# A pair's value row is added one pair later on VectorE, behind the dots of the next pair

## Chip, cores and metric

One core of one Trainium2 chip. The metric is the device time of one execution in microseconds (us); a kernel's time is the median of its runs.

## The reference

One layer over 512 latent tokens of width 1024 (and 256 context tokens): a token mixer, then an expert mixer (PEER). All in float32. The change lies in the expert mixer, whose core is, for each block of 128 tokens `xb`:

```python
q = (xb @ w_q).reshape(T, 8, 2, 128)
s = jnp.einsum('thpd,hpnd->thpn', q, keys)      # scores against 2 x 128 keys for each of 8 heads
sv, si = lax.top_k(s, 16)
cand = sv[:, :, 0, :, None] + sv[:, :, 1, None, :]
cv, ci = lax.top_k(cand.reshape(T, 8, 256), 16)
eid = i1 * 128 + i2                             # i1, i2: taken from si by ci // 16 and ci % 16
g = jax.nn.softmax(cv, axis=-1)
u = jnp.take(u_tab, eid, axis=0)
act = jax.nn.gelu(jnp.einsum('thkd,td->thk', u, xb))
out = jnp.einsum('thk,thkd->td', g * act, jnp.take(v_tab, eid, axis=0))
```

So each token picks 8 x 16 = 128 experts. Of each it needs a row `u` (1024 numbers), dotted with the token, and a row `v`, added to the output with the weight gate x gelu(dot). The block is followed by a norm, a scaling and the residual.

## The kernel before

**Tiling.** The 512 tokens are four blocks t of 128, one token on each of the 128 partitions. A step n from 0 to 511 is one expert of each token of a block (128 steps in a block). A pair j = 0 to 255 is the steps 2j (even) and 2j + 1 (odd). `BT` = 64 pairs make a block, `BP` = 16 pairs make a group of two heads.

**Gathers.** The tables u and v lie side by side in memory, so that GpSimd's one indirect DMA for a step (L613) fetches row u and row v of each of the 128 tokens: 8 KB on each partition, 1.049 MB in all. They go into a ring of six slots (`NGS`, `gslot`), step n into slot n % 6; the ring holds three pairs. GpSimd issues the steps in order. Before step n it waits until the row of step n - 6 in its slot is used up: for an even step on `s_vadd` (VectorE has added that row, L612), for an odd one on `s_peused` (TensorE has multiplied it).

**One pair, engine by engine.** VectorE (`pick(j)`) waits for the landing of each row (`landed`) and takes its dot with the token (L1642), one instruction for a row. ScalarE (its own `pick(j)`) waits for both dots, takes gelu (L1128), multiplies by the gate into `wexp` (L1133, two instructions), and builds a diagonal matrix from the odd step's weight (L1138). TensorE (`add_row`, L917) multiplies the odd row v by that matrix in four column pieces and sums over the block in two banks. VectorE waits for the even step's weight (`s_wexp`) and adds the even row v times the weight to `vacc` (L1657; L1654 for the first of a block). The even values are thus summed by VectorE, the odd ones by TensorE. At the end of a block `products(t)` adds the two sums: ScalarE copies TensorE's sums to `vbuf` (L1145), VectorE adds `vacc` (L1668).

**Ranking.** The next groups' experts are picked by VectorE in small steps. `rank(g)` is a generator; `pick(j)` takes four of its steps in each of the first 12 pairs of a group of 16, between the dots and the add, for the group two further on. No group is left to be ranked from pair 240 on.

**Order.** A list `BSEQ` is written out ahead, and each engine runs its own part of each entry in that order: ("pk", j) is a pair, and behind it, for j below 112, stand side steps: the query projections of the expert mixer (L887, with ScalarE's copies L1101 and others) and the late half of the token mixer (L671, L707, L856), whose weights SyncE loads through a ring of four buffers. ScalarE and TensorE too take all of this in order, so that a pair can stand behind a side step. From pair 112 on there are only pairs, ranking and the ends of blocks.

Of the kernel before, what the change touches and what calls it, by code (L numbers as in the profile page):

```python
# [28 lines left out]
def build(nc, x, ctx_in, rows_a, rows_b, w_ada, w_in, w_dt, conv_w, dt_bias, a_log, d_skip, w_out, w_q, keys,  # L29
# [110 lines left out]
    BT = NE // 2  # L140
# [105 lines left out]
    with ExitStack() as stack:  # L246
# [180 lines left out]
        def landed(eng, n):  # L427
            eng.wait_ge(s_gsl[n % NGS], 16 * (n // NGS + 1))

        def row_u(n):  # L430
            return gslot[n % NGS][:, 0:D]

        def row_v(n):
            return gslot[n % NGS][:, D:2 * D]
# [765 lines left out]
        def _(dve):  # L1200
# [12 lines left out]
            def link(ins):  # L1213

                post(ins)
                settle()
# [418 lines left out]
            def pick(j):  # L1635

                nonlocal ranking
                t = j // BT
                for n in (2 * j, 2 * j + 1):
                    landed(dve, n)  # L1640
                    k = n % NE
                    V.tensor_tensor_reduce(row_u(n), row_u(n), h2[t], 1.0, 0.0, ALU.mult, ALU.add,  # L1642
                                           dots[:, k:k + 1]).then_inc(s_dot, 1)
                g = j // BP + 2
                if j % BP < 12 and g < len(groups):
                    if j % BP == 0:
                        ranking = rank(g)
                    for _ in range(4):
                        next(ranking, None)
                n = 2 * j  # L1650
                w = wexp[:, n % NE:n % NE + 1]
                dve.wait_ge(s_wexp, n + 1)
                if j % BT == 0:
                    V.tensor_scalar(vacc, row_v(n), w, None, ALU.mult).then_inc(s_vadd, 1)  # L1654
                else:
                    dve.wait_ge(s_vadd, j)
                    V.scalar_tensor_tensor(out=vacc, in0=row_v(n), scalar=w, in1=vacc,  # L1657
                                           op0=ALU.mult, op1=ALU.add).then_inc(s_vadd, 1)
# [4 lines left out]

            def products(t):

                dve.wait_ge(s_vcp, t + 1)
                dve.wait_ge(s_vadd, (t + 1) * BT)
                link(V.tensor_tensor(vbuf, vbuf, vacc, ALU.add))  # L1668
# [20 lines left out]
            def late_squares(ct):  # L1689
# [3 lines left out]
                else:  # L1693
                    dve.wait_ge(s_sqaB, ct)
                    V.tensor_tensor(sqacc[1], sqacc[1], sq[1], ALU.add).then_inc(s_sqaB, 1)

            parts = {"rank": rank_end, "norm": gate_norm, "pk": pick, "vs": products, "fin": finish,
                     "zy": late_z, "gn": group_scale, "conv": lambda ct: conv(ct, 1),
                     "gate": lambda ct: gated(ct, 1), "sqa": late_squares, "yT": y_drain, "ss": lambda: sc_sum(1),
# [48 lines left out]
```

## Time and profile before

| | us |
|---|---|
| runs of the kernel | 2097.53, 2096.0, 2109.05 |
| median | 2097.53 |
| profiled execution: first to last instruction (span) | 2089.7 |
| VectorE busy | 1491.0 (71%) |
| TensorE matmul busy | 1518.5 (73%) |
| GpSimd busy | 878.6 (42%) |
| ScalarE busy | 497.1 (24%) |

The profiled execution's own device time is not listed apart from its span; the nearest of the runs, 2096.0, is 6.3 us above that span. The share of busy time is a mean over very different stages: the mixer up to about 583 us, then the expert phase. "Idle before" in a row of the page is the time in which the engine did nothing just ahead of such an instruction, with what ended most of it. Busy time of the DMA engines is a share of all 16.

### The profile page before, as it was taken

What the parts mean: (1) busy time and instruction counts of PE and PEld (TensorE: products, weight loads), DVE (VectorE), ACT (ScalarE), POOL (GpSimd) and SP (SyncE); (2) the same over time, 40 slices, a digit from 0 to 9 for tenths busy, and PEclk for the clock granted to TensorE, in tenths of its full rate; (3) what the DMA queues carried; (4) which work ended last, traced back from release to release, by engine and by line L of the source; (5) the groups of instructions that cost most, each with busy time, mean ns of one, the idle gap of its engine ahead of it and who ended that gap; (6) DMA issues with size and microseconds to landing.
All of it is one profiled execution on the core that took longest, in us unless ns stands there. A gap on an engine that the chain in (4) does not pass through costs nothing.

```text
span 2089.7 us, 15934 instructions
## 1 busy us (share of the span) xinstructions
PE 1518.5 (73%) x4648; PEld 876.7 (42%) x4648; DVE 1491.0 (71%) x2906; ACT 497.1 (24%) x1412; POOL 878.6 (42%) x658
## 2 busy tenths in 40 slices
PE   7899999889667778887865778655555555556564
PEld 3465787668545555564531445311111111111111
DVE  2545368763276667878598856688898898898876
ACT  2201120111222233223233322222222223222222
POOL 2478404220033333343345434345554555455553
PEclk9899899999879899999987899877777767676677
DMA  8233221124278999999999999799999999999997
GB/s 348 101 139 138 89 79 61 62 77 144 81 308 353 362 351 345 410 392 387 421 393 361 386 378 347 282 413 387 413 412 422 403 409 387 409 417 409 406 418 294
DMA packets 90604, 647.28 MB, mean 310 GB/s; under 512 B 10413, under 2 KB 10773, under 8 KB 12565
## 3 DMA queue, kind: packets, MB, share of 16 engines
q0 software_dynamic: 76448, 555.78, 66.7%
q1 hardware_dynamic: 13376, 90.25, 11.2%
q8 instruction: 38, 0.62, 0.1%
q14 instruction: 49, 0.40, 0.1%
q10 hardware_dynamic: 693, 0.23, 0.0%
HBM read 644.12 MB, written 2.10 MB: 309 GB/s over the span
## 4 chain that ended last, share of the span: by engine, by line
PE 42%; DMA 21%; DVE 19%; issue 8%; ACT 7%; POOL 2%; SPq 0%; DVEq 0%; ACTq 0%; POOLq 0%
DMA arena<-in_peer_uv,arena 21%; PE bank L917 13%; PE bank L671 11%; DVE arena L1642 6%; PE bank L887 6%; PE bank L856 4%; DVE arena L1657 3%; PE bank L707 3%; POOL arena L613 2%; ACT smalls L1138 2%; ACT arena L1133 1%; ACT arena L1128 1%; PE bank L906 1%; PE bank L697 1%; PE bank L800 1%
## 5 line engine op out<-in xcount | busy, mean ns | idle before, releaser
L613 POOL DMA_INDIRECT arena<-in_peer_uv,arena x512 | 688.8, 1345 | 901.4 <-DVE arena L1657 571.1
L917 PE MATMUL bank<-arena,smalls 128*128 128x512 f32 x1024 | 700.9, 822 | 477.6 <-ACT smalls L1138 470.7
L1642 DVE CUSTOM_DVE_ANT_0 arena<-arena 128x1024 f32<-128x1024 f32 x512 | 615.1, 1221 | 87.5 <-DMA arena<-in_peer_uv,arena 86.1
L917 PEld LDWEIGHTS bank<-arena,smalls 128*128 128x128 f32 x1024 | 225.7, 241 | 887.8 <-ACT smalls L1138 675.2
L1657 DVE SCALAR_TENSOR_TENSOR arena<-arena 128x1024 f32<-128x1024 f32 x252 | 322.0, 1278 | 204.8 <-ACT arena L1133 204.8
L671 PE MATMUL bank<-arena 128*128 128x256 f32 (+1 forms) x1216 | 336.1, 433 | 3.6 <-ACT arena L962 3.4
L671 PEld LDWEIGHTS bank<-arena 128*128 128x128 f32 x1216 | 235.9, 195 | 104.6 <-issue 76.0
L1128 ACT ACTIVATE arena<-arena 128x2 f32<-128x2 f32 x256 | 51.9, 203 | 778.0 <-DVE arena L1642 776.3
L887 PE MATMUL bank<-arena 128*128 128x256 f32 x512 | 125.4, 402 | 0.7 <-issue 0.7
L1133 ACT ACTIVATE arena<-arena 128x1 f32<-128x1 f32 x512 | 122.9, 287 | 8.5
L887 PEld LDWEIGHTS bank<-arena 128*128 128x128 f32 x512 | 106.2, 208 | 35.9 <-issue 21.5
L856 PE MATMUL bank<-arena 128*128 128x256 f32 x512 | 114.5, 382 | 1.9 <-DVE arena L1493 1.6
L856 PEld LDWEIGHTS bank<-arena 128*128 128x128 f32 x512 | 98.1, 192 | 23.3 <-issue 10.7
L1138 ACT ACTIVATE smalls<-ident,arena 128x128 f32<-128x128 f32 x256 | 102.8, 401 | 8.4
L533 POOL TENSOR_TENSOR arena<-arena,cs 128x2048 f32<-128x2048 f32 x16 | 58.3, 3641 | 52.0 <-PE bank L679 43.2
L1280 DVE TENSOR_SCALAR arena<-bank,early 128x512 f32<-128x512 f32 (+1 forms) x28 | 18.4, 693 | 82.3 <-PE bank L671 82.3
L1262 DVE SCALAR_TENSOR_TENSOR arena<-bank,early,arena 128x496 f32<-128x496 f32 (+1 forms) x112 | 62.6, 622 | 0.6
L707 PE MATMUL bank<-arena 128*128 128x256 f32 x256 | 60.9, 398 | 0.0
L707 PEld LDWEIGHTS bank<-arena 128*128 128x128 f32 x256 | 52.1, 204 | 12.3 <-issue 5.0
L556 POOL TENSOR_TENSOR arena<-arena 128x256 f32<-128x256 f32 x7 | 5.4, 776 | 95.2 <-DVE arena L1394 95.2
L968 ACT ACTIVATE arena<-arena 128x512 f32<-128x512 f32 x16 | 10.1, 630 | 148.1 <-DVE arena L1262 148.1
L1500 DVE TENSOR_TENSOR arena<-bank,arena 128x512 f32<-128x512 f32 x8 | 5.5, 688 | 54.6 <-ACT arena L1058 54.6
(241 smaller groups left out, 1311.5 us busy)
## 6 DMA issues: line engine op xcount, KB each, us to landing
arena<-in_w_in SPq DMA_DIRECT2D x40, 1024.0 KB, 6.2
arena<-in_w_ada POOLq DMA_DIRECT2D x16, 1024.0 KB, 5.1
arena<-in_w_out SPq DMA_DIRECT2D x16, 1024.0 KB, 6.8
arena<-in_peer_w_q SPq DMA_DIRECT2D x16, 1024.0 KB, 9.9
arena<-in_w_ada SPq DMA_DIRECT2D x8, 1024.0 KB, 9.2
arena<-in_peer_uv,arena POOLq DMA_INDIRECT x512
arena<-in_x SPq DMA_DIRECT2D x4, 512.0 KB, 11.3
out<-arena SPq DMA_DIRECT2D x4, 512.0 KB
```

The costliest lines, as they stand in the source:

```text
L613: nc.gpsimd.indirect_dma_start(gslot[n % NGS], None, uv_tab[0], bass.IndirectOffsetOnAxis(eid[t % 2][:, k:k + 1], 0)).then_inc(s_gsl[n % N ...
L671: last = mm(dst, w[:, k, j * P:(j + 1) * P], hT(k), start=(k == 0), stop=(k == KD - 1))
L707: last = mm(ps[:, i * WCOL:(i + 1) * WCOL], hT_tile(halves[half][i], k), w[:, k, :], start=(k == 0), stop=(k == KD - 1))
L856: last = mm(ps[:, i * WCOL:(i + 1) * WCOL], src[:, k, i * P:(i + 1) * P], w[:, k, :], start=(k == 0), stop=(k == KD - 1))
L887: last = mm(ps[:, i * WCOL:(i + 1) * WCOL], h2T[:, m % NA, k, :], w[:, k, :], start=(k == 0), stop=(k == KD - 1))
L917: last = mm(acc[h][:, :], diag[:, j % NDG], row_v(n)[:, h * 512:(h + 1) * 512], start=(i == 0), stop=(i == BT - 1))
L1128: A(gelu[:, k:k + 2], dots[:, k:k + 2], ACT.Gelu_apprx_tanh).then_inc(s_gelu, 1)
L1133: A(wexp[:, k + i:k + i + 1], gate[t % 2][:, k + i:k + i + 1], ACT.Copy, scale=gelu[:, k + i:k + i + 1]).then_inc(s_wexp, 1)
L1138: A(diag[:, j % NDG], ident[:], ACT.Copy, scale=wexp[:, k + 1:k + 2]).then_inc(s_diag, 1)
L1262: return V.scalar_tensor_tensor(out=d, in0=s, scalar=w, in1=d, op0=ALU.mult, op1=ALU.add)
L1642: V.tensor_tensor_reduce(row_u(n), row_u(n), h2[t], 1.0, 0.0, ALU.mult, ALU.add, dots[:, k:k + 1]).then_inc(s_dot, 1)
L1657: V.scalar_tensor_tensor(out=vacc, in0=row_v(n), scalar=w, in1=vacc, op0=ALU.mult, op1=ALU.add).then_inc(s_vadd, 1)
```

## The change

In `pick(j)` of VectorE the last part, the wait for the weight and the add of the even value row, becomes a function of its own, `add_value(j)`. `pick(j)` calls it for the pair before, j - 1, behind its own dots and ranking steps; the first pair of a block calls nothing. The last pair of a block is added at the start of `products(t)`. The arithmetic and the other engines' programs stay as they are.

```diff
                         ranking = rank(g)
                     for _ in range(4):
                         next(ranking, None)
+                if j % BT:
+                    add_value(j - 1)
+
+            def add_value(j):
+
                 n = 2 * j
                 w = wexp[:, n % NE:n % NE + 1]
                 dve.wait_ge(s_wexp, n + 1)
...
             def products(t):
 
+                add_value((t + 1) * BT - 1)
                 dve.wait_ge(s_vcp, t + 1)
                 dve.wait_ge(s_vadd, (t + 1) * BT)
                 link(V.tensor_tensor(vbuf, vbuf, vacc, ALU.add))
```

## Rows read from the trace of the kernel before

**Rows 1.** The page: the DMA share in 40 slices (tenths), and two costly groups.
```profile
DMA  8233221124278999999999999799999999999997
L613 POOL DMA_INDIRECT arena<-in_peer_uv,arena x512 | 688.8, 1345 | 901.4 <-DVE arena L1657 571.1
L1657 DVE SCALAR_TENSOR_TENSOR arena<-arena 128x1024 f32<-128x1024 f32 x252 | 322.0, 1278 | 204.8 <-ACT arena L1133 204.8
```

**Rows 2.** Stage windows: start:end, length, each engine's busy us (instructions), clock, DMA share, GB/s.
```profile
core 0: us, PE busy (x) PEld busy (x) DVE busy (x) ACT busy (x) POOL busy (x), PEclk, DMA share, GB/s
583.00:1348.00 765.00, 574.64 (x1896) 365.17 (x1896) 557.68 (x1130) 220.78 (x622) 305.46 (x233) 0.89 0.94 369
1348.00:2078.00 730.00, 425.42 (x565) 132.90 (x564) 624.49 (x1196) 184.16 (x602) 383.08 (x280) 0.72 0.99 405
900.00:1050.00 150.00, 121.88 (x433) 81.49 (x432) 112.57 (x233) 40.23 (x124) 53.28 (x46) 0.94 0.99 408
```

**Rows 3.** Windows of L1642 alone (two records a dot), then of L1657 alone.
```profile
583.00:1348.00 765.00, 274.26 (x459) 0.89 0.94 369
1348.00:2078.00 730.00, 343.78 (x566) 0.72 0.99 405
1348.00:2078.00 730.00, 177.72 (x140) 0.72 0.99 405
```

**Rows 4.** Waits in 1350 to 2078 us: total us, times, longest.
```profile
POOL arena L613 <- DVE arena L1657: 220.0, 128, 4.9
POOL arena L613 <- PE bank L917: 84.3, 76, 2.2
DVE arena L1642 <- DMA arena<-in_peer_uv,arena: 60.8, 93, 2.2
DVE arena L1657 <- ACT arena L1133: 38.4, 64, 0.7
```

**Rows 5.** Waits in 583 to 1350 us.
```profile
DVE arena L1657 <- ACT arena L1133: 166.4, 67, 9.2
ACT arena L1101 <- PE bank L887: 115.4, 14, 9.5
```

**Rows 6.** Timeline of the last pairs: start, length, instruction, [idle before, releaser].
```profile
2062.79 1.28 DVE L1657 SCALAR_TENSOR_TENSOR arena<-arena 128x1024 f32<-128x1024 f32 x1 [0.60 <-ACT arena L1133]
2064.35 1.68 POOL L613 DMA_INDIRECT arena<-in_peer_uv,arena  x1 [1.34 <-DVE arena L1657]
2065.92 1.23 DVE L1642 CUSTOM_DVE_ANT_0 arena<-arena 128x1024 f32<-128x1024 f32 x1 [0.70 <-DMA arena<-in_peer_uv,arena]
2067.23 0.94 POOL L613 DMA_INDIRECT arena<-in_peer_uv,arena  x1 [1.21 <-PE bank L917]
2075.95 1.22 DVE L1642 CUSTOM_DVE_ANT_0 arena<-arena 128x1024 f32<-128x1024 f32 x1 [0.61 <-DMA arena<-in_peer_uv,arena]
2081.11 1.23 DVE L1668 TENSOR_TENSOR arena<-arena 128x1024 f32<-128x1024 f32 x1 [2.05 <-ACTq L1147]
```

**Rows 7.** The chain of waits, 1500 to 1530 us: start, length, what.
```profile
1505.21 9.45 DMA arena<-in_peer_uv,arena
...
1521.03 8.65 DMA arena<-in_peer_uv,arena
```

**Rows 8.** An issue with idle DMA engines (timeline), and windows behind it (POOL only).
```profile
1336.03 1.68 POOL L613 DMA_INDIRECT arena<-in_peer_uv,arena  x1 [4.88 <-DVE arena L1657]
...
1335.00:1338.00 3.00, 1.68 (x1) 1.00 0.00 0
1338.00:1339.00 1.00, 0.95 (x1) 1.00 0.73 131
1338.00:1344.60 6.60, 2.93 (x3) 1.00 0.84 310
```

**Rows 9.** A quick issue, its first bytes, and the last bytes of all (as rows 8).
```profile
1312.30 0.94 POOL L613 DMA_INDIRECT arena<-in_peer_uv,arena  x1 [6.34 <-DVE arena L1657]
...
1313.00:1314.00 1.00, 0.25 (x1) 0.50 0.24 41
2075.00:2076.00 1.00, 0.00 (x0) 0.50 0.02 8
```

## The prediction

> **What bounds the kernel now.** I read the page first: the busy shares by slice, then the costliest groups [rows 1]. From slice 12 on the DMA engines are at nine or ten tenths, and what they carry is the 512 indirect gathers. The same page says that GpSimd, which issues them, sat idle 901.4 us in front of them and that 571.1 us of this ended with VectorE's value add (L1657). So the add is not just arithmetic: it hands back the slot into which the next gather goes. Then the stage windows [rows 2]. The expert phase has two parts: one in which other projections run beside it (583 to 1348 us) and one of gathers alone (1348 to 2078 us). In the second the DMA share is 0.99 at 405 GB/s; VectorE is busy 624.5 of 730 us, 86%. There are 283 dots in it [rows 3], 141.5 pairs, so a pair takes 730 / 141.5 = 5.16 us; two gathers of 1.049 MB at 405 GB/s take 5.18 us. **The second part runs at the speed of the transfers**, with VectorE close behind. The first part has 229 dots, 114.5 pairs of 6.68 us.
>
> The waits of the second part [rows 4] say what the change can remove: VectorE's add waits 38.4 us for ScalarE's weight, 0.6 us at a time, and this time is idle time of an engine that next waits 60.8 us for a landing. Taking 38 us out of it makes the other wait longer. In the first part the add waits 166.4 us [rows 5].
>
> **How deep the queue is.** The timeline of the last pairs [rows 6] is plain enough to number the gathers backwards from 511. Gather 510 (even, the next to last) is issued at 2064.35, 0.28 us after the end of the add of pair 252 (2062.79 + 1.28), whose even slot it takes. The odd one, 511, is issued at 2067.23 and its dot starts at 2075.95, having waited for it: 8.7 us. The chain of waits shows the same stretch elsewhere, issue to odd dot, at 9.45 and 8.65 us [rows 7]. What would it be with nothing ahead in the queue? At 1336.03 a gather is issued while the engines stand still [rows 8]. They stay at 0.00 until 1338 and are at 0.73 in the next microsecond: about 2.2 us of start-up (I count from 1338.25). A transfer is 2.6 us, and from the last bytes, somewhere in 2075 to 2076 at a share of 0.02 [rows 9], to the dot are some tenths; with the thin tail before them I count 0.7 us. Together 5.5 us. So an odd gather has 8.7 - 5.5 = 3.2 us to spare. Even 510 has landed by 2075.9 less one transfer, 2073.3, which is 9.0 us after its issue and leaves 3.5 us.
>
> **The change, part by part.** No instruction is added or removed: 256 adds stay 256. What moves is the order on VectorE.
> - The add of pair j now stands behind both dots of pair j+1 and the ranking steps put there. Add 252 (2062.79 to 2064.07) would come behind the odd dot of pair 253, which starts at 2065.92 because it waits for a landing: it would end at 2065.92 + 1.23 + 1.28 = 2068.43, **4.36 us later**, more where ranking steps stand between. Spare are 3.2 to 3.5 us. The slot comes back too late, by about 1 us even with no ranking, and the cover that now hides the whole latency of a gather is gone. Of six slots (three pairs) one pair more is held.
> - Queued behind it: the gather of an even row waits for this add on GpSimd's queue, and the odd row's gather stands behind it in that queue. TensorE has released the odd slot long before, which now helps nothing: POOL's 84.3 us behind L917 [rows 4] turn into waits for L1657.
> - VectorE's wait for the weight goes to about nothing, since ScalarE has the next two dots' time for it. Worth 0: late next is the landing.
> - At three block ends and at the very end the last add is done in `products`, behind the one that is late: one add (1.28 us) more there, 4 times 1.28 = 5 us without cover. The cover is ScalarE's copy of TensorE's sums, for which VectorE stood idle 2.05 us before it summed `vbuf` at 2081.11 [rows 6]: 0.
> - ScalarE and TensorE keep their order. The dots come before the add now, so ScalarE gets them 1.9 us sooner where data has already landed; in the second part it has not.
>
> **The sum, second part.** The new loop spans two pairs: landing of the odd row of j+1, its dot, ranking, add j, issue for pair j+3, transfer, landing of j+3. Terms: dot 1.23 [rows 6]; ranking 0.73 (VectorE's busy 624.5 less dots 343.8 less adds 177.7 [rows 2, 3] is 103.0, over 141.5 pairs, block ends counted in); add 1.28; GpSimd's answer 0.28; start-up 2.2; two transfers at 405 GB/s 5.18; notice 0.7. Sum 11.60 us for two pairs, **5.80 us a pair**. Start-up, which the present loop hides, is bounded from both sides. After the quick issue of 1312.30 (0.94 us long) first bytes come at about 1313.76, a share of 0.24 in that microsecond [rows 9]: 1.46 us, and 5.43 us a pair. After the slow issue of 1336.03 (1.68 us) the bytes of both rows are in at 1344.6, 8.6 us, where start-up and two transfers at full rate would be 7.4 [rows 8]: engines that ran dry climb slowly. With that the two pairs take 12.8 us, 6.41 us each. I take 5.85: GpSimd's issue will stand beside VectorE's next dot, as at 1336.03, so the slow start is the nearer row, but at 6.41 us the engines would hardly run dry and there would be little to climb. Cost: (5.85 - 5.16) x 141.5 = **98 us**, ends 38 and 177.
>
> That fixed part has a page too. The Trainium skill, DMA: Bandwidth & Descriptors, section Anatomy of one DMA, fits a DMA issued by GpSimd as 2.0 us plus its bytes at 436 GB/s. An estimate from it is 4.4 us for one gather, against the 5.5 above, and the loop would be about 5.3 us a pair, near rival 1. The rows show more than 2.0 us for start-up alone after a slow issue, so I go by them.
>
> **First part.** Per pair 6.68 us, and weights share the engines. In 900 to 1050 us the share is 0.99 with 46 gathers [rows 2], 23 pairs of 6.5 us; 408 GB/s x 150 us less 48.2 MB of rows leaves 13 MB, 0.54 weight loads a pair. Over two pairs that is 2.8 us of DMA, half of it inside the loop: 11.6 + 1.4 = 13.0, 6.5 us a pair. The loop is as long as the pair already is: uneven pairs lose, the mean hardly. Where TensorE and ScalarE set the pace (the engines stand idle from 1335 to 1338 [rows 8]), gathers land early and a late release costs nothing. I take 0.25 us on 114.5 pairs: **29 us**, ends 0 and 80 (0.7 us, what the second part loses).
>
> Sum: 98 + 29 = 127 us on the profiled span of 2089.7, 2217. The runs lie 6.3 us and more above that span, the median 7.8 above; so 2097.5 + 127 = **2225 us**.
>
> **Rivals.**
> 1. *The fixed part of a gather is smaller (no change).* With start-up at 1.46 and notice at 0.2, the loop is 1.23 + 0.73 + 1.28 + 0.28 + 1.46 + 5.18 + 0.2 = 10.36, 5.18 us a pair: nothing is lost, and the time stays at 2097 to 2100. For: the quick start of rows 9, and the 9.45 us of rows 7, which leave 4.0 to spare. Against: the 8.65 beside it, the slow issue beside a dot, and ranking in 12 of 16 pairs. The Trainium skill's fit, named above, comes within 0.1 us a pair of this.
> 2. *Faster: VectorE's waits were on the path.* In the first part L1657 waits 166.4 us for ScalarE [rows 5], up to 9.2 us. With dots ahead of the add, gelu, diagonal and TensorE's product come sooner. If a quarter of the 166.4 shortens the path and the second part holds, 2097.5 - 42 = 2056. It decides if the loop over two pairs stays under 10.3 us (2 x 5.16). Against: the long waits are ScalarE standing behind TensorE's query halves in its own order (ACT L1101 waits 115.4 us for L887), which dots done sooner don't move.
> 3. *Every pair pays the ramp, the first part too.* 177 + 80 = 257: 2355 us. Against: a loop that long no longer runs dry.
> 4. *The change doesn't do what it says.* Only if the order of the dots and the add came out as before; the add is a call behind the ranking steps, so it does not. No chance of its own.
>
> **How the numbers follow.** Forecast (a loop of 5.4 to 6.4 us a pair in the second part, some loss in the first) 0.80; rival 3 or beyond 0.09; rival 1 0.07; rival 2 0.04. Low: 38 + 0 gives 2135, taken as 2130. High: the second part's upper end and half of the first's, 177 + 40, gives 2315, taken as 2320. One per cent, 21 us, is about what a measurement here can tell from no change. Faster by over 1% 0.04, within 1% 0.07, slower by over 1% 0.89.
>
> **What would show it.** In the second part: a pair every 5.8 us; DMA share near 0.88 instead of 0.99 and GB/s near 360; GpSimd's wait for L1657 up from 220 us toward 350 and its wait for L917 gone; VectorE's wait for the landing (L1642) up from 61 us to some 150, its wait for ScalarE gone; issue to odd dot near 6 us rather than 8.7 to 9.5. In the first part: a span from 765 to about 795 us. The prediction is wrong if the DMA share of the second part stays at 0.99, or if the first part takes most of the loss.

## The result: 2391 us, 14% slower

| kernel | median us | runs | ratio to before (95% interval) |
|---|---|---|---|
| before | 2096.8 | 2092.9 to 2109.05 | |
| with the change | 2391.2 | 2384.6 to 2399.2 | 1.1395 (1.1354 to 1.1437) |

The forecast was 2225 us, the range 2130 to 2320. The sign and the place were right. The size was not: 294 us lost, where 127 were forecast and 223 were the most that the range allowed.

The page of the changed kernel (the group's fields are as in [rows 1]; the add is now L1662):

```profile
DMA  8243212242898988898889888888888888888886
q0 software_dynamic: 76448, 555.78, 62.6%
L613 POOL DMA_INDIRECT arena<-in_peer_uv,arena x512 | 620.0, 1211 | 1267.3 <-DVE arena L1662 1041.0
L1642 DVE CUSTOM_DVE_ANT_0 arena<-arena 128x1024 f32<-128x1024 f32 x512 | 625.1, 1225 | 549.2 <-DMA arena<-in_peer_uv,arena 547.2
L1662 DVE SCALAR_TENSOR_TENSOR arena<-arena 128x1024 f32<-128x1024 f32 x252 | 321.4, 1276 | 6.2 <-ACT arena L1133 5.8
```

Nothing is dearer on VectorE (the add 1276 ns, before 1278). Its wait for ScalarE fell from 204.8 to 5.8 us, and its wait for landings, 60.8 us in the second part before [rows 4], is 547.2 us over the whole kernel. GpSimd waits 1041.0 us for the add instead of 571.1 [rows 1].

By parts, in windows of the same columns as [rows 2]. Pair 112 starts its dots at 1406.5 us here, at 1335.7 us before; the last pair at 2374.8 and 2074.1.

```profile
583.00:1411.00 828.00, 599.70 (x1870) 373.27 (x1869) 558.11 (x1127) 216.47 (x608) 270.08 (x228) 0.84 0.88 335
1411.00:2378.00 967.00, 493.67 (x596) 156.11 (x594) 638.19 (x1211) 188.32 (x613) 349.90 (x285) 0.65 0.85 311
```

The second part's DMA share is 0.85 at 311 GB/s, against 0.99 at 405. TensorE's granted clock fell too, from 0.72 to 0.65, while TensorE was busy for 51% of the second part instead of 58%. With the dots' starts as marks, the time went here:

| | pairs | us a pair before | after | us in all |
|---|---|---|---|---|
| up to the first dot | | | | +4.1 |
| first part | 112 | 6.65 | 7.24 | +66.7 |
| second part | 143 | 5.16 | 6.77 | +229.9 |

Together 300.7 of the 301.4 us between the two spans. The waits of the second part, beside [rows 4]:

```profile
POOL arena L613 <- DVE arena L1662: 547.6, 138, 7.5
DVE arena L1642 <- DMA arena<-in_peer_uv,arena: 315.4, 220, 4.0
POOL arena L613 <- issue: 38.7, 127, 0.3
```

GpSimd's wait for TensorE is gone from the list, as forecast; the odd gather follows the even one at once. So TensorE's lower clock holds up no gather here. The timeline shows the loop over two pairs, at a pair without ranking steps (rows between left out):

```profile
2253.62 1.23 DVE L1642 CUSTOM_DVE_ANT_0 arena<-arena 128x1024 f32<-128x1024 f32 x1 [2.46 <-DMA arena<-in_peer_uv,arena]
...
2254.77 1.28 DVE L1662 SCALAR_TENSOR_TENSOR arena<-arena 128x1024 f32<-128x1024 f32 x1
...
2256.32 0.95 POOL L613 DMA_INDIRECT arena<-in_peer_uv,arena  x1 [4.35 <-DVE arena L1662]
...
2257.57 1.78 POOL L613 DMA_INDIRECT arena<-in_peer_uv,arena  x1 [0.30 <-issue]
...
2259.76 1.23 DVE L1642 CUSTOM_DVE_ANT_0 arena<-arena 128x1024 f32<-128x1024 f32 x1 [1.21 <-DMA arena<-in_peer_uv,arena]
...
2264.75 1.23 DVE L1642 CUSTOM_DVE_ANT_0 arena<-arena 128x1024 f32<-128x1024 f32 x1 [2.57 <-DMA arena<-in_peer_uv,arena]
...
2267.23 1.23 DVE L1642 CUSTOM_DVE_ANT_0 arena<-arena 128x1024 f32<-128x1024 f32 x1 [1.25 <-DMA arena<-in_peer_uv,arena]
```

The odd dot at 2253.62 belongs to some pair j + 1. The add of pair j follows it, the even gather of pair j + 3 goes out at 2256.32, 2.7 us behind the dot's start, and the odd dot of pair j + 3 starts at 2267.23, having waited: 10.9 us behind the issue. Two pairs took 13.6 us. At 2259.76, 3.4 us after that issue, the pair j + 2, issued one turn earlier, has only just come in. Over pairs 112 to 239 (up to 240 a later group is still ranked, in 12 pairs of each 16) the timeline gives, as means, 3.53 us from odd dot to even issue, the release, and 10.07 us from even issue to odd dot, the delivery: 13.6 us, 6.81 us a pair. With six slots in this order the two add up to two pair times by the way they are counted, so the sum is no test; what moves each of them is.

### The profile page after: what moved, and what is told of

Read it like the earlier page. It is cut to its first block, busy times and chain, and to the rows that moved or that the text cites. A ratio compares the mean times of both kernels' runs of the same rounds, so it can differ in the third digit from the quotient of the medians.

```text
span 2391.1 us, 15934 instructions
## 1 busy us (share of the span) xinstructions
PE 1615.3 (68%) x4648; PEld 909.8 (38%) x4648; DVE 1503.3 (63%) x2906; ACT 497.5 (21%) x1412; POOL 809.8 (34%) x658
## 3 DMA queue, kind: packets, MB, share of 16 engines
q0 software_dynamic: 76448, 555.78, 62.6%
## 4 chain that ended last, share of the span: by engine, by line
DMA 40%; PE 24%; DVE 18%; issue 9%; POOL 6%; ACT 3%; POOLq 0%; SPq 0%; DVEq 0%; ACTq 0%
DMA arena<-in_peer_uv,arena 39%; PE bank L671 10%; POOL arena L613 6%; DVE arena L1662 5%; PE bank L917 4%; DVE arena L1642 3%; PE bank L856 2%; PE bank L887 2%; PE bank L707 1%; PE bank L697 1%; DVE arena L1602 1%; PE bank L800 1%; DVE arena L1233 1%; PE bank L786 1%; PE bank L636 1%
## 5 line engine op out<-in xcount | busy, mean ns | idle before, releaser
L917 PE MATMUL bank<-arena,smalls 128*128 128x512 f32 x1024 | 787.2, 912 | 682.0 <-ACT smalls L1138 681.8
L613 POOL DMA_INDIRECT arena<-in_peer_uv,arena x512 | 620.0, 1211 | 1267.3 <-DVE arena L1662 1041.0
L1642 DVE CUSTOM_DVE_ANT_0 arena<-arena 128x1024 f32<-128x1024 f32 x512 | 625.1, 1225 | 549.2 <-DMA arena<-in_peer_uv,arena 547.2
L917 PEld LDWEIGHTS bank<-arena,smalls 128*128 128x128 f32 x1024 | 251.0, 268 | 1146.8 <-ACT smalls L1138 916.4
L1662 DVE SCALAR_TENSOR_TENSOR arena<-arena 128x1024 f32<-128x1024 f32 x252 | 321.4, 1276 | 6.2 <-ACT arena L1133 5.8
L671 PEld LDWEIGHTS bank<-arena 128*128 128x128 f32 x1216 | 238.3, 197 | 107.4 <-issue 77.9
L887 PE MATMUL bank<-arena 128*128 128x256 f32 x512 | 128.6, 409 | 0.7 <-issue 0.7
L887 PEld LDWEIGHTS bank<-arena 128*128 128x128 f32 x512 | 108.4, 212 | 37.1 <-issue 21.7
L856 PE MATMUL bank<-arena 128*128 128x256 f32 x512 | 115.3, 383 | 1.9 <-DVE arena L1493 1.6
L856 PEld LDWEIGHTS bank<-arena 128*128 128x128 f32 x512 | 99.0, 194 | 24.6 <-issue 11.9
L1262 DVE SCALAR_TENSOR_TENSOR arena<-bank,early,arena 128x496 f32<-128x496 f32 (+1 forms) x112 | 62.6, 621 | 0.6
L707 PE MATMUL bank<-arena 128*128 128x256 f32 x256 | 62.6, 406 | 0.0
L707 PEld LDWEIGHTS bank<-arena 128*128 128x128 f32 x256 | 53.3, 208 | 13.3 <-issue 5.5
L1642 DVE DVE_READ_ACCUMULATOR2_ANT arena<- 128x1 f32 x512 | 42.3, 83 | 0.0
L968 ACT ACTIVATE arena<-arena 128x512 f32<-128x512 f32 x16 | 10.1, 631 | 148.2 <-DVE arena L1262 148.2
```

The costliest lines, as they stand in the source:

```text
L613: nc.gpsimd.indirect_dma_start(gslot[n % NGS], None, uv_tab[0], bass.IndirectOffsetOnAxis(eid[t % 2][:, k:k + 1], 0)).then_inc(s_gsl[n % N ...
L671: last = mm(dst, w[:, k, j * P:(j + 1) * P], hT(k), start=(k == 0), stop=(k == KD - 1))
L707: last = mm(ps[:, i * WCOL:(i + 1) * WCOL], hT_tile(halves[half][i], k), w[:, k, :], start=(k == 0), stop=(k == KD - 1))
L856: last = mm(ps[:, i * WCOL:(i + 1) * WCOL], src[:, k, i * P:(i + 1) * P], w[:, k, :], start=(k == 0), stop=(k == KD - 1))
L887: last = mm(ps[:, i * WCOL:(i + 1) * WCOL], h2T[:, m % NA, k, :], w[:, k, :], start=(k == 0), stop=(k == KD - 1))
L917: last = mm(acc[h][:, :], diag[:, j % NDG], row_v(n)[:, h * 512:(h + 1) * 512], start=(i == 0), stop=(i == BT - 1))
```

## The experiments

Theory A is the prediction's: the slot comes back too late, too few gathers are under way, and two pairs take release plus delivery. Rival B: the new order itself costs, through ScalarE, TensorE or slower transfers, however early slots come free. Every kernel's second part is described by two numbers from its timeline, the time of a pair (from the start of pair 112's even dot to the last pair's) and the delivery, the mean time from a pair's even issue to its odd dot over pairs 112 to 239. Where a time of a pair is called one of pairs 112 to 239, it is the mean over the same pairs. Each of these numbers is from one profiled execution.

**1. Ranking behind the add.** In the changed kernel:

```diff
+                if j % BT:
+                    add_value(j - 1)
                 if j % BP < 12 and g < len(groups):
                     ...
                         next(ranking, None)
-                if j % BT:
-                    add_value(j - 1)
```

> The changed order, but the four ranking steps of a pair stand behind the add of the pair before: dots j, add j-1, ranking j. Theory A (the release of the even slot is late, and two pairs take the path from the odd dot to the gather's issue, 3.53 us as measured in the changed kernel, plus 10.07 us from that issue to the odd dot two pairs on): the path gets 0.73 us shorter, a ranked pair of the second part goes from 6.81 to 6.45 us, 46 us less there, some 20 to 25 less in the first part, in all about 2320 us. Rival B (the new order itself slows ScalarE, TensorE or the transfers, however early the slot is released): no change, 2391 us.

Measured: 2293.7 us, ratio 1.093 (1.089 to 1.098). The release path fell from 3.53 to 2.72 us, the delivery took 9.92 us, a pair of 112 to 239 took 6.32 us. The test is that the delivery hardly moved while the release got 0.81 us shorter. The gain is 97 us, where 66 to 71 were expected: the second part got 6.77 - 6.33 = 0.44 us a pair shorter, 64 us, and the first part 0.27 us, 31 us. Moving some 0.8 us of ranking from ahead of the add to behind it was worth 97 us. That speaks against B.

**2. The add between the dots.**

```diff
                     V.tensor_tensor_reduce(row_u(n), ...).then_inc(s_dot, 1)
+                    if n % 2 == 0 and j % BT:
+                        add_value(j - 1)
...
-                if j % BT:
-                    add_value(j - 1)
```

> The add of pair j-1 stands between the even dot and the odd dot of pair j, ranking behind both. Theory A: from the even dot, 1.23 + 1.28 + 0.28 = 2.8 us to the issue, plus 7.3 us from issue to even dot as measured in the changed kernel, 10.1 us for two pairs: 5.05 us a pair, so the transfers bound again at about 5.2 us; 2391 - 143 x 1.6 = 2160 us or less, the first part perhaps near before too, 2100. Rival B: the add is still a pair late and behind a dot of the next pair; most of the loss stays, over 2300 us.

Measured: 2176.7 us, ratio 1.040 (1.036 to 1.044). Most of the loss is gone, but a pair takes 5.65 us, not 5.05 to 5.2. The miss is in the delivery: from even issue to even dot it was 8.64 us here, where I had carried over the 7.3 us of the changed kernel. With the issue coming earlier, more is still under way ahead of it: by the trace's records of single DMA packets (packet records below) the first bytes of an even gather come 3.64 us behind its issue here, 2.40 us in the changed kernel (means over pairs 112 to 239). Delivery is not a constant.

**3. The old order with four slots.**

```diff
-        gslot = [at(k, 2 * D) for k in (56, 64, 72, 80, 88, 96)]
+        gslot = [at(k, 2 * D) for k in (56, 64, 72, 80, 88, 96)[:4]]
```

> The kernel before (old order) with four slots in the ring instead of six. Theory A (what counts is how many gathers are under way): the even path is like the changed kernel's, 3.5 us, the odd one is later since TensorE releases its slot some 6.3 us behind the odd dot, plus 8.3 to 8.9 us from odd issue to odd dot: 14.9 us for two pairs, 7.4 a pair in the second part, 320 us more than before there, perhaps 100 in the first: about 2520 us. Rival B (the order is what costs): well under 2250 us.

Measured: 2427.3 us, ratio 1.158 (1.153 to 1.164). With the order untouched and one pair fewer in the ring, the second part takes 6.78 us a pair, nearly the changed kernel's 6.77. The number is below the 2520 expected, because odd gathers came 7.2 us behind their issue (mean of pairs 112 to 239), not 8.3 to 8.9. So the loss needs no new order: a lost pair in the ring is enough.

**4. The changed order with ten slots in the second part.** The core of the edit:

```diff
-        gslot = [at(k, 2 * D) for k in (56, 64, 72, 80, 88, 96)]
-        NGS = len(gslot)
+        gslot = [at(k, 2 * D) for k in (56, 64, 72, 80, 88, 96) + (0, 8, 16, 24)[:4]]
+        NGS, N0 = 6, 228
+        NEXT = len(gslot)
+        later = list(range(NGS, NEXT)) + [(N0 - NGS + i) % NGS for i in range(NGS)]
+        slots = [n % NGS if n < N0 else later[(n - N0) % NEXT] for n in range(NPK)]
+        uses = [slots[:n].count(slots[n]) for n in range(NPK)]
+        prior = [max((i for i in range(n) if slots[i] == slots[n]), default=None) for n in range(NPK)]
...
-                if n >= NGS:
-                    if n % 2:
-                        pool.wait_ge(s_peused, (n - NGS) // 2 + 1)
-                    else:
-                        pool.wait_ge(s_vadd, (n - NGS) // 2 + 1)
+                if n == N0:
+                    await_filled(pool, ("q", *units[-1]))
+                if prior[n] is not None:
+                    pool.wait_ge(s_peused if prior[n] % 2 else s_vadd, prior[n] // 2 + 1)
```

> The changed order with the ring grown from six to ten slots from step 228 on (the four buffers of the weight ring, 8 KB a partition each, are free by then); the first part keeps six. Theory A: four pairs share the path of 13.6 us, the transfers bound again, the second part returns from 6.77 to 5.16 us a pair: 230 us less, 2160 us. Rival B: no change in the second part, 2391 us.

Measured: 2147.1 us, ratio 1.025 (1.021 to 1.030). The same windows, first the changed order with ten slots, then experiment 5's kernel:

```profile
1411.00:2124.00 713.00, 411.87 (x580) 132.35 (x580) 622.49 (x1202) 185.19 (x604) 401.62 (x283) 0.75 1.01 419
```

```profile
1345.00:2060.00 715.00, 412.04 (x576) 130.31 (x576) 626.96 (x1209) 186.20 (x607) 402.39 (x282) 0.75 1.00 417
```

A pair takes 5.08 us, less than before the change, with every add still behind the next pair's dots. At this depth the changed order costs 0.06 us a pair against the old one (5.02 us, experiment 5), where at six slots it costs 1.61. So the second part's loss came through the ring, all but a few microseconds, and B falls. The granted clock is back at 0.75, so its fall went with the slower pace. What is left against before is the first part, which kept six slots (7.28 us a pair).

**5. The old order with ten slots.** The edit of experiment 4 in the kernel before.

> The kernel before (old order) with the ring grown from six to ten slots from step 228 on. If the second part is held by the transfers alone (DMA share 0.99), nothing changes: 2097 us. If three pairs in the ring leave small gaps, a pair goes from 5.16 us toward 4.95 us (what two gathers take at the 424 GB/s of the best stretches): 30 us less, 2067 us.

Measured: 2077.5 us against 2096.6 on the same chip, ratio 0.991 (0.988 to 0.993), a small gain with 1 outside the interval. A pair takes 5.02 us. So the second part of before was not held by the transfers alone: a share of 0.99 at 405 GB/s still had 0.14 us a pair in it, which a deeper queue (417 GB/s) takes back.

**6. The changed order with four slots.** The slots of experiment 3 in the changed kernel.

> The changed order with four slots: a pair's gathers are issued only when both dots of the next pair are done, so nothing else is under way when they start. This measures by itself what two gathers take from the first issue to the odd dot on engines at rest. A pair is 3.5 us + that time. If the prediction's sum was right (start-up 2.2, two transfers 5.18, notice 0.7 = 8.1): 11.6 us a pair, about 3560 us. If the dry stretch at 1336 us of before was the right price (8.6 + 0.7 = 9.3): 12.8 a pair, 3870 us. If the 10.07 us of the changed kernel is a price of engines at rest, and not of the pair ahead still under way: 13.6, about 4080 us.

Measured: 3768.2 us, ratio 1.799 (1.793 to 1.805). One pair's delivery onto engines at rest, in the timeline and in windows of GpSimd alone (columns as in [rows 8]):

```profile
3601.57 0.94 POOL L613 DMA_INDIRECT arena<-in_peer_uv,arena  x1 [9.90 <-DVE arena L1662]
3602.81 0.94 POOL L613 DMA_INDIRECT arena<-in_peer_uv,arena  x1 [0.30 <-issue]
3607.04 1.23 DVE L1642 CUSTOM_DVE_ANT_0 arena<-arena 128x1024 f32<-128x1024 f32 x1 [5.75 <-DMA arena<-in_peer_uv,arena]
3610.02 1.23 DVE L1642 CUSTOM_DVE_ANT_0 arena<-arena 128x1024 f32<-128x1024 f32 x1 [1.74 <-DMA arena<-in_peer_uv,arena]
```

```profile
3600.00:3603.00 3.00, 1.13 (x2) 0.50 0.00 0
3603.00:3605.00 2.00, 0.75 (x1) 0.50 0.89 246
3605.00:3609.00 4.00, 0.00 (x0) 0.50 0.94 389
3609.00:3610.00 1.00, 0.00 (x0) 0.50 0.12 49
```

First bytes come 1.6 us behind the issue (by the packet records at 3603.21; 1.64 us is also the median over the quick issues, under 1 us long, of pairs 112 to 239), then the engines are at a share of 0.89 but move only 246 GB/s for two microseconds, and the last bytes trickle in behind 3609. Over pairs 112 to 239 the mean is 5.70 us to the even dot and 8.96 us to the odd one. By the packet records the 8.96 us are 1.73 to the first bytes, 6.89 until both gathers have landed, and 0.34 until the dot starts. The forecast's 8.1 us was too little even for engines at rest, the 9.3 us of the dry stretch in before slightly too much. And 10.07 us, the price in the changed kernel, is not a price of engines at rest. The 1.1 us more are put down to the pair ahead, which lands there 2.9 us (mean) after the even issue, when the new gather could already be moving. Slow issues are not the reason: in the changed kernel pairs with two quick issues took 10.11 us, the others 10.01. The Trainium skill, DMA: Bandwidth & Descriptors, Anatomy of one DMA, would give 2.0 + 2 x 1.049 MB at 436 GB/s = 6.8 us as an estimate for these two gathers; the measured 8.96 decides.

**7. Bursts of four on engines at rest**, in the kernel before (the label is bursts_of_four):

```diff
+                if n and n % 4 == 0:
+                    pool.wait_ge(s_vadd, n // 2)
                 if n >= NGS:
```

> The order of before with six slots, but GpSimd waits ahead of every fourth gather until all adds before it are done: four gathers go out onto engines at rest. It measures what each gather behind the first costs. In after_four_slots the even dot came 5.63 us behind the issue, the odd one 3.3 us later, though the full rate is 2.5 us a gather. If only the first step behind rest is slow, the dots come at about 5.6, 8.9, 11.4 and 13.9 us, and the time is near 2850 us; if every step is, at 5.6, 8.9, 12.2, 15.5, and the time is near 3030 us.

Measured: 3037.0 us, ratio 1.448 (1.443 to 1.454). The time fits the second case, and yet the windows of a burst issued at 2518.85 say the first:

```profile
2519.00:2520.00 1.00, 0.79 (x1) 0.50 0.00 0
2520.00:2522.00 2.00, 1.60 (x2) 0.80 0.75 193
2522.00:2531.00 9.00, 1.23 (x2) 0.62 1.00 400
2531.00:2533.00 2.00, 0.00 (x0) 0.50 0.26 107
```

Four gathers (4.19 MB) are in by about 2532.2, 13.4 us behind the issue, where 13.9 and 15.5 were the two cases. Over all bursts of pairs 112 to 239 the packet records say the same: the four gathers have landed 5.28, 8.58, 11.05 and 13.53 us behind the first issue. The second costs 3.3 us behind the first, the third and fourth 2.5 each. Slow are two microseconds at the start and one at the end; between them the rate is 400 GB/s. My total of 2850 us was wrong because VectorE, ranking for both pairs and adding both, comes on top: the dots start 5.64, 8.93, 12.57 and 14.14 us behind the first issue, and two pairs took 17.9 us in the second part. The total told nothing; the windows did.

**8. The changed order with eight slots** in the second part, by experiment 4's edit with `[:2]` for `[:4]`, so two slots more than six.

> The changed order with eight slots from step 228 on. Theory C, from the runs so far (pairs under way = time from even issue to odd dot, over time of a pair: 0.72 gives 12.4 us a pair, 1.48 gives 6.81, 1.97 gives 5.65, 2.25 gives 5.17, 3.2 gives 5.08): the time of a pair hangs on the number under way and bends slowly toward 5.0. Three pairs share a path of which 3.5 us is release: with 5.15 us a pair 2.3 pairs are under way, which fits the curve; second part 5.15, in all 2391 - 143 x 1.62 = 2160 us. A sharp bend (a pair takes the larger of 5.03 us and a third of 3.5 + 8.9 = 12.4 us) would give 5.03 and 2143 us.

Measured: 2155.5 us, ratio 1.028 (1.024 to 1.032), 5.10 us a pair, delivery 11.8 us. Theory C said 2160 us and 5.15, the sharp bend 2143 and 5.03. The time is nearer to C and the interval (2147 to 2164 us) leaves the other out, but not by much; the clearer case for a bend is experiment 2. Theory C was added with this run, after the miss of experiment 2. Pairs under way are delivery over time of a pair:

| kernel | slots, order | delivery us | us a pair, 112 to 239 | pairs under way |
|---|---|---|---|---|
| after_four_slots | 4, changed | 8.96 | 12.41 | 0.72 |
| bursts_of_four | 6, old, in fours | 10.27 | 9.00 | 1.14 |
| before_four_slots | 4, old | 9.76 | 6.81 | 1.43 |
| after | 6, changed | 10.07 | 6.81 | 1.48 |
| rank_behind_add | 6, ranking behind | 9.92 | 6.32 | 1.57 |
| add_between_dots | 6, between | 11.16 | 5.65 | 1.98 |
| mixed_order_six_slots | 6, mixed (below) | 11.61 | 5.23 | 2.22 |
| before | 6, old | 11.63 | 5.17 | 2.25 |
| after_eight_slots | 8, changed | 11.77 | 5.12 | 2.30 |
| after_ten_slots | 10, changed | 16.42 | 5.08 | 3.23 |
| mixed_order_ten_slots | 10, mixed (below) | 20.85 | 5.08 | 4.11 |
| before_ten_slots | 10, old | 20.78 | 5.02 | 4.14 |

Whatever the order and the ring, the time of a pair goes with the last column. The column is worked out with the time of a pair, so within one kernel the two are tied; what speaks is that kernels of different orders and rings which agree in it agree in the time (6.81 and 6.81 at 1.43 and 1.48, 5.23, 5.17 and 5.12 at 2.22 to 2.30). Below two pairs under way the time falls steeply; from 2.3 on little is left. The corner is not sharp: with two pairs under way, 10 us of transfers, a pair takes 5.65 us and not 5.0. In the ten-slot kernels rows also lie landed while VectorE is busy, and the delivery counts this: by the packet records the odd gather has landed 16.4 us behind the even issue in before_ten_slots and 13.4 in after_ten_slots, so 3.3 and 2.6 pairs were really in transfer.

**9 and 10. A mixed order.** The add stands between the dots of the next pair beside the query projections (pairs 0 to 17 and 88 to 111), else behind its own dots; once with ten slots in the second part, once with six throughout.

```diff
                 for n in (2 * j, 2 * j + 1):
+                    if n % 2 and owed is not None:
+                        add_value(owed)
+                        owed = None
                     landed(dve, n)
...
+                owed = j
+                if not (j < 18 or UB <= j < len(side)) or j % BT == BT - 1:
+                    add_value(j)
+                    owed = None
```

> Ten slots from step 228 on as in before_ten_slots, and in the pairs beside query projections (0 to 17 and 88 to 111) the add of pair j stands between the dots of pair j+1, elsewhere behind its own dots as before. In add_between_dots those stretches took 6.76 and 6.49 us a pair instead of 7.06 and 6.93: there VectorE's wait for ScalarE is on the path. Gain 18 x 0.30 + 24 x 0.44 = 16 us beside the ring's 19: about 2061 us. If the gain there came from slots that were late elsewhere in that kernel, nothing: 2077 us.

> The same mixed order with the six slots of before. If the order is worth something beside the query projections: 2097 - 16 = 2081 us. If not: 2097 us.

Measured: 2074.7 us, ratio 0.990 (0.988 to 0.992), and 2098.4 us, ratio 1.000 (0.999 to 1.002). With six slots the two stretches did get shorter in the profile, to 6.78 and 6.55 us a pair from 7.06 and 6.93, some 14 us; the rest of that profile got longer by about as much (late projections, pairs 18 to 75, 6.73 for 6.67; pairs 76 to 87, without side steps but for the last two, 5.54 for 5.38; second part 5.21 for 5.16), and the median moved by nothing. Where these microseconds go back is not settled: the profile is one execution. With ten slots the mixed order lies within the interval of experiment 5, so no gain beside the ring's is shown.

## Why the prediction was right in sign and wrong in size

- **What bounds the second part: right, but too sharp.** The transfers bound it; experiment 5 found 0.14 us a pair still in the ring.
- **The release path: right.** 1.23 + 0.73 + 1.28 + 0.28 = 3.52 us forecast, 3.53 us measured, and experiment 1 moved it and the time with it. That the slot would come back too late, and one pair of three be lost, held as well (experiments 3 and 4).
- **The step that failed: "start-up 2.2; two transfers at 405 GB/s 5.18; notice 0.7", 8.1 us.** It measured 10.07, and the 2 us that were missing are of two kinds. At rest it is 8.96 (experiment 6): start-up 1.73 and notice 0.34 are both less than forecast, but two transfers took 6.89 us from first bytes to landing and not 5.18, since a gather onto idle engines starts at 246 GB/s and its tail thins out. I had taken a throughput (405 GB/s of a full queue) for a duration. The other 1.1 us goes with the pair ahead, whose odd dot starts 3.4 us after the even issue (2259.76 against 2256.32): the new gathers stand behind it.
- **The weighing was wrong where it had the number.** The dry stretch [rows 8] gave 8.6 us for start-up and both transfers, and with notice 9.3, or 6.41 us a pair. (Even that was read too low: the packet records have the last bytes of both rows at 1345.88, 9.8 us behind the issue, and the bytes up to 1344.6 were short of both rows. The two first bytes were read 0.2 us early: 1313.96 and 1338.42.) I set it aside as "at 6.41 us the engines would hardly run dry". They do: a share of 0.85, and both things at once, a queue to stand in and engines that are partly idle. The reason for leaning to the slow start failed too: most even issues of the changed kernel's second part were quick (median 0.95 us). The upper end left out the pair ahead: 3.5 us of release and 9.0 of delivery at rest are 6.2 us a pair, and with 10.1 it is 6.8.
- **The middle, 5.85 us a pair, took the loop as if nothing stood in its way.** Nothing was added for loop and transfers coming out close together, 5.80 against 5.18 us. The table shows a wide bend there: 5.65 us at two pairs under way, where transfers alone allow 5.02.
- **The first part: right in kind, too small.** 29 us forecast with ends 0 and 80, 67 measured (7.24 for 6.65 us a pair); of these some 51 us fell on the pairs beside the late projections, 7.55 for 6.67. The loop of 13.0 us measured 14.6: in the changed kernel's timeline the release is 3.57 us and the delivery 11.06 (means over pairs 6 to 111), where 3.5 and 9.5 had been summed. No run tried this part by itself, and the granted clock fell there too, from 0.89 to 0.84; what that cost is open.
- **Rivals.** No change (start-up 1.46, notice 0.2): the quick start was there, 1.64 us behind the issue at rest, and did not help. The fit of the Trainium skill's DMA: Bandwidth & Descriptors (Anatomy of one DMA), 4.4 us for one gather, stands against 5.70 measured at rest, so that rule would have led to this rival. Faster: there was something in it, the stretches beside query projections were 0.30 and 0.44 us a pair faster with the add between the dots, but no total was shown to gain by it. Rival 3, every pair pays the ramp, was the nearest: 2355 us. Its doubt, that a loop that long no longer runs dry, was unfounded.
- **What would show it.** Forecast for the second part: share 0.88, 360 GB/s, GpSimd's wait 350 us, VectorE's 150, issue to odd dot near 6. Measured: 0.85, 311, 547.6, 315.4, and 8.5 (mean from odd issue; 9.3 before). All in the named direction; the first four went further than forecast, the last not nearly as far, which is the failed step seen in another place. The window of the first part is 828 us, where about 795 was forecast.

## What to carry to other kernels

Before you move an instruction that frees a buffer, count the transfers under way (time from issue to use, over time of a step) with the new order, and look up what the kernel does at that count; here the wait of 199 us that the change took from VectorE was worth nothing beside that. Price a delivery by a measured issue-to-use time at the same depth, not by bytes over the best rate. When loop and transfers come out nearly equal, expect a step to take longer than either, as at two pairs under way here (5.65 us against 5.02). If such a reorder is wanted, give the ring the slots first: with ten slots the late add cost 0.06 us a pair in the second part instead of 1.61, and the old order with ten slots beat the kernel before by 0.9%.

## What the runs showed of the hardware that was not expected

- A pair of 1.049 MB gathers onto resting engines takes 8.96 us from first issue to use, 12.41 us a pair with release, though ten slots deliver a pair every 5.02 us.
- For about two microseconds behind the first bytes the engines are at a share of 0.75 to 0.89 and move 193 to 246 GB/s, where later a share of 1.00 moves 400. In after_four_slots a packet of 8 KB takes 0.82 us on average in the first quarter of a microsecond and 0.31 us from 1.5 us on. Over the whole kernel the same 76448 packets took 62.6% of 2391.1 us after the change and 66.7% of 2089.7 before, 1497 against 1394 us: 7% longer each. The slow first packets go with this; why they are slow was not tried.
- GpSimd's issue got shorter by itself (1211 ns for 1345, 970 ns in after_four_slots), and this was worth nothing beside the rest. It goes with the dots beside it: issues that share over 0.5 us with a dot took 1601 ns on average before (282 of them) and 1412 ns after (247), those that share nothing 1046 and 1033 ns; in after_four_slots none stands beside a dot.
